# Block 2: when the low part of the next query's weights is made, and both modulation rows ahead of the first value pair

## What is computed

```python
for i in range(DEPTH_2):
    sh, sc, gt = jnp.split(jax.nn.silu(c) @ ada_w[i] + ada_b[i], 3, axis=-1)
    h = rms_norm(x, norm_g[i]) * (1.0 + sc[:, None]) + sh[:, None]
    u, z = jnp.split(h @ w_in, [n_mix_cols], axis=-1)
    o, oc = mixer(u, uc, ...)
    x = x + gt[:, None] * ((o * jax.nn.silu(z)) @ w_out)
```

## Time and profile before

| | us |
|---|---|
| median of 3 runs (lowest, highest) | 2190.47 (2190.22, 2192.97) |
| the profiled execution: time, span | 2195.91, 2194.1 |
| PE busy | 1974.0 (90%) |
| DVE busy | 1199.5 (55%) |
| ACT busy | 1098.0 (50%) |
| POOL busy | 985.2 (45%) |
| block 2, layers 0, 1, 2, 3: from, us | 935, 1209, 1577, 1963 |

### The profile page before, as it was taken

How to read it: one execution, slowest core, us unless ns; L and a number is a source line. 1 busy time by engine, 2 the same in 40 slices (tenths; PEclk the granted TensorE clock), 3 DMA queues, 4 the chain that set the end, 5 groups by cost and what they waited for, 6 DMA issues and landing times.

```text
span 2194.1 us, 39543 instructions
## 1 busy us (share of the span) xinstructions
PE 1974.0 (90%) x14720; PEld 1675.1 (76%) x14720; DVE 1199.5 (55%) x2584; ACT 1098.0 (50%) x2101; POOL 985.2 (45%) x616
## 2 busy tenths in 40 slices
PE   6899899998999899969998899899879989977897
PEld 5798789988898899946776697666569666656676
DVE  5854556657654466435775304677340766723574
ACT  5353465444543665454554526454443555644563
POOL 0474468303754485024453443344234545533563
PEclk8899999998999999979999999899999989989998
DMA  7343556564444565543112422322232211123222
GB/s 258 113 148 106 176 173 188 183 200 131 132 126 148 178 194 185 176 158 105 50 49 78 163 87 77 103 72 62 93 125 87 70 66 49 49 91 119 80 87 59
DMA packets 72994, 262.93 MB, mean 120 GB/s; under 512 B 8048, under 2 KB 10224, under 8 KB 72560
## 3 DMA queue, kind: packets, MB, share of 16 engines
q1 hardware_dynamic: 71536, 256.31, 36.5%
q0 software_dynamic: 1280, 4.20, 0.6%
HBM read 259.43 MB, written 1.05 MB: 119 GB/s over the span
## 4 chain that ended last, share of the span: by engine, by line
PE 67%; DVE 14%; issue 6%; ACT 6%; POOL 5%; DMA 1%; SPq 0%; DVEq 0%; ACTq 0%; POOLq 0%
PE gemm L494 16%; PE gemm L495 15%; PE gemm L496 15%; PE score L852 2%; DVE pr L1940 2%; DVE small L1903 2%; PE stat L739 2%; POOL w_parts L327 2%; PE obank L925 1%; PE gemm L792 1%; POOL rot L2124 1%; PE gemm L793 1%; PE gemm L794 1%; PE gemm L702 1%; ACT pr L1460 1%
## 5 line engine op out<-in xcount | busy, mean ns | idle before, releaser
L327 POOL TENSOR_TENSOR w_parts<-ring,w_parts 128x1024 fp32r<-128x1024 f32 x280 | 672.8, 2406 | 709.7 <-ACT w_parts L1112 698.7
L1112 ACT ACTIVATE w_parts<-ring 128x1024 fp32r<-128x1024 f32 x364 | 382.6, 1054 | 136.0 <-PE gemm L496 63.3
L494 PE MATMUL gemm<-g_hi,w_parts 128*128 128x256 f32 x1344 | 396.1, 295 | 28.5 <-DVE w_parts L327 10.7
L494 PE MATMUL gemm<-h_hi,w_parts 128*128 128x512 f32 (+1 forms) x928 | 379.8, 409 | 14.9 <-ACTq L1352 6.8
L495 PE MATMUL gemm<-g_lo,w_parts 128*128 128x256 f32 x1344 | 385.7, 287 | 0.0
L496 PE MATMUL gemm<-g_hi,w_parts 128*128 128x256 f32 x1344 | 385.1, 287 | 0.0
L495 PE MATMUL gemm<-h_lo,w_parts 128*128 128x512 f32 (+1 forms) x928 | 352.0, 379 | 0.0
L496 PE MATMUL gemm<-h_hi,w_parts 128*128 128x512 f32 (+1 forms) x928 | 351.5, 379 | 0.0
L494 PEld LDWEIGHTS gemm<-g_hi,w_parts 128*128 128x128 f32 x1344 | 265.4, 197 | 47.6 <-issue 24.0
L495 PEld LDWEIGHTS gemm<-g_lo,w_parts 128*128 128x128 f32 x1344 | 264.8, 197 | 0.1
L496 PEld LDWEIGHTS gemm<-g_hi,w_parts 128*128 128x128 f32 x1344 | 264.3, 197 | 0.0
(11 more groups left out here) (328 smaller groups left out, 3972.3 us busy)
## 6 DMA issues: line engine op xcount, KB each, us to landing
ring<-wall SPq DMA_DIRECT2D x478, 512.0 KB, 3.7
r<-nbias POOLq DMA_DIRECT2D x16, 256.0 KB, 3.0
cst<-consts SPq DMA_DIRECT2D x1, 2037.0 KB, 13.4
r<-x_t SPq DMA_DIRECT2D x1, 1024.0 KB, 5.7
x<-ctx_t SPq DMA_DIRECT2D x1, 1024.0 KB, 15.7
y_t<-x SPq DMA_DIRECT2D x4, 256.0 KB, 3.0
cst<-consts SPq DMA_DIRECT2D x1, 303.5 KB, 3.1
x<-pos SPq DMA_DIRECT2D x1, 128.0 KB, 2.1
```

What stands on the lines that cost most here:

```text
L327: eng.tensor_tensor(w_lo[:, at, :, :], ring[:, t % RING, :, :], w_hi[:, at, :, :].bitcast(F), ALU.subtract)\
L494: pe.matmul(out, w[0][:, k, :], x[0], start=start, stop=False)
L1112: act.activation(w_hi[:, at, :, :], ring[:, t % RING, :, :], ACT.Copy).then_inc(S["hi_ready"], 1)
```

## The change

1. `hi_parts` is called on ACT right behind the first pair's exponentials, for the query tile two ahead; before, that high part came with the query's copy at the second pair. Kinds A and B.
2. POOL waits before the low part of that tile until the first pair of the current chunk has been normalised.
3. In the last layer normalisation ACT no longer makes high parts of the two value tiles between the modulation rows; in layer 0 they come behind the exponential's square.
4. At the start of each layer all rows (two in layer 0, one after) are made ahead of value pair 0, in banks ob and tb and not in gemm banks, and so are the columns. ACT copies the rows behind the last high part of h. The first key sum and the first scores wait for the columns' copies.

The tile numbers, as a function that ACT and POOL share:

```diff
+        def qz_tile(L, i):
+            return AT["qz", L] + i + (4 if i >= 4 else 0) if FILL_SLOT[L] else AT["qz", L] + i + 1
```

On PE, in `block2`:

```diff
-                run(ada_row())
+                for r in range(FILL_RMS[L]):
+                    run(ada_row((ob, tb)[r]))
...
                     if j == 0:
-                        for _ in range(FILL_RMS[L] - 1):
-                            run(ada_row())
-                        for _ in range(FILL_RMS[L]):
-                            ada_columns()
+                        for r in range(FILL_RMS[L]):
+                            ada_columns((ob, tb)[r])
```

On ACT (`ada_columns_out` gets the same argument `at`):

```diff
-            def ada_row_out(ahead=AHEAD):
-                b = op(4, None, ahead)
+            def ada_row_out(ahead=AHEAD, at=None):
+                if at is None:
+                    b = op(4, None, ahead)
+                else:
+                    b = at
+                    n["tile"] += 4
+                    act.wait_ge(slot_used[(n["tile"] - 1) % RING], (n["tile"] - 1) // RING + 1)
...
                 for _ in range(FILL[i]):
-                    ada_row_out()
+                    ada_row_out(AHEAD if first else 0)
...
                 act.activation(zh[:, 0, :], rstd[:, :], ACT.Square).then_inc(S["rstd_ready"], 1)
+                if L == 0:
+                    hi_parts(n["tile"] + 1)
                 n["tile"] += 2
-                ada_row_out(0)
...
                     if L and m == KC - 3:
-                        hi_parts(n["tile"])
+                        hi_parts(n["tile"] + 4)
                 high(KC - 1)
+                for r in range(FILL_RMS[L]):
+                    ada_row_out(0, (ob, tb)[r])
...
                     if j == 0:
-                        for _ in range(FILL_RMS[L] - 1):
-                            ada_row_out()
-                        for _ in range(FILL_RMS[L]):
-                            ada_columns_out()
+                        for r in range(FILL_RMS[L]):
+                            ada_columns_out((ob, tb)[r])
...
                         exponential(c, u)
                         exponential(c, u + 1)
+                        if u == 0:
+                            hi_parts(qz_tile(L, 2 * c + 3))
```

On POOL, in `block2`:

```diff
                 def q_side(c):
-                    split_to(qz_tile(2 * c + 1) if c else AT["k", L] + 1)
+                    if c and kind != "C":
+                        pool.wait_ge(S["p_normed"], pbase(L) + (c - 1) * NU + 2)
+                    split_to(qz_tile(L, 2 * c + 1) if c else AT["k", L] + 1)
```

More of the change, by code:

```diff
@@ L762, in ones_head @@
                         pe.wait_ge(S["v_ready"], vbase(L) + nk)
+                        pe.wait_ge(S["ada_evac"], n["ada"])
                     if j == 1:
@@ L1121, in ada_row_out, with ada_columns_out @@
                 seq(ins)
-                act.sem_inc(S["bank_read"], 1)
+                if at is None:
+                    act.sem_inc(S["bank_read"], 1)
                 act.sem_inc(S["ada_row"], 1)
                 n["row"] += 1
-            def ada_columns_out():
+            def ada_columns_out(at=None):
                 r = n["ada"]
@@ L1129, in ada_columns_out @@
                 act.wait_ge(S["ada_col"], r + 1)
-                b = op(0)
+                b = op(0) if at is None else at
                 seq(act.activation(ada[:, :, :, :].rearrange("p l m v -> p (l m v)")[:, r * 8:(r + 1) * 8], b[:, 0:8], ACT.Copy))
-                act.sem_inc(S["bank_read"], 1)
+                if at is None:
+                    act.sem_inc(S["bank_read"], 1)
                 act.sem_inc(S["ada_evac"], 1)
@@ L2212, in block2 @@
                     pool.tensor_scalar(h2[:, m, T:N2], h2[:, m, T:N2], mod[:, m, 1:2], ada[:, L, m, 1:2], ALU.mult, ALU.add).then_inc(S["h_ctx"], 1)
-                def qz_tile(i):
-                    return AT["qz", L] + i + (4 if i >= 4 else 0) if FILL_SLOT[L] else AT["qz", L] + i + 1
                 def q_side(c):
-                    split_to(qz_tile(2 * c + 1) if c else AT["k", L] + 1)
+                    if c and kind != "C":
+                        pool.wait_ge(S["p_normed"], pbase(L) + (c - 1) * NU + 2)
+                    split_to(qz_tile(L, 2 * c + 1) if c else AT["k", L] + 1)
                     if kind != "B":
@@ L2244, in block2 @@
                 for c in range(KC):
-                    split_to(qz_tile(2 * c + 2))
+                    split_to(qz_tile(L, 2 * c + 2))
                     if not FILL_SLOT[L]:
```

## The result

The changed kernel takes 2171.08 us (median of five runs, 2169.15 to 2178.43) for 2190.47; the ratio is 0.9911, interval 0.9894 to 0.9927. Six more executions, beside 24 of the kernel before, gave a median of 2173.69 us and 0.9929 (0.9901 to 0.9957).

The account below looks back on a forecast made before the run. TensorE, busy for most of a chunk, was held by normalisation waits in layers 0 and 1 and a pause at layer 0's start. 2.0 + 5.5 + 3.3 + 2.4 = 13.2 us off 2190.47 gave 2177.3 us, range 2173.5 to 2183.5.

Parts of the forecast that it names:

- the start of layer 0: Both modulation rows first: squares 3.0 us earlier, value pair 0 later, no pause before query 0; −3.3 us together.
- the rival in which the clock returns early: Row matmuls lift PE's clock before value pair 0 in layer 0: 2.6 us more gain, 2174.7 us, chance 0.12.
- the columns: Layers 1 to 3: columns no longer wait 0.8 us for a copied gemm bank; −2.4 us in sum.
- which edit acts where: Attention loops: high part with low part behind bias loads in layer 1, both edits in layer 0, wait alone in chunk 1.
- The margin in layer 1: The second L1940 of a chunk ends 0.2 us before PE asks for it.
- the two loop terms: Gains from removed PE waits in the attention loops: 2.0 us in layer 0 and 5.5 us in layer 1.
- All six waits go (five of 0.2 and one of 0.9): −2.0 us: Layer 0's attention: PE's turn no longer waits for the normalisation; bounds 0 and 2.0 us.
- The five waits of 1.1 us go whole: −5.5 us: Layer 1's attention: PE's turn no longer waits for the second normalisation; bounds 2.8 and 5.5 us.
- the slower rival: Layer 3: low part released only by the second pair's normalisation, PE idles 3.1 us, clock falls; 2208 us, chance 0.03.
- the rivals with a gain: Early clock (0.12), slower ring at layer 0's start (0.13), layer 1's wait kept (0.06), loop edits without effect (0.03).
- the upper bound of both terms: Most the loop edits could gain: 2.0 us in layer 0, 5.5 us in layer 1.
- ACT's order doesn't change: Layer 3: only POOL's low part moves, 0.3 us later, covered by a gap of 3.1 us; cost 0.

Follow-up runs that it names:

- e2: The changed kernel with the attention loop of the kernel before, so only rows first, banks ob and tb, and columns: 2190.18 us, ratio 0.9996.
- e8: The changed kernel plus two extra VectorE operations between the second pair's two normalisations, chunks 2 to 6 of layer 1, so PE waits there again: 2175.35 us.
- e4: The kernel before with only POOL's wait for the first pair's normalisation added, the high part left at the second pair: 2187.55 us.
- e3: The kernel before with only ACT's high part moved to the first pair, without POOL's wait for the normalisation: 2180.90 us.
- e9: The changed kernel plus one extra VectorE operation between the second pair's two normalisations, chunks 2 to 6 of layer 1: 2170.62 us.
- e1: The kernel before with both attention loop edits (earlier high part, POOL's wait) and rows and columns as before: 2179.20 us, ratio 0.9957.
- e7: The changed kernel with POOL's low part in layer 3 waiting for the second pair's normalisation instead of the first's: 2191.16 us.

## Why the prediction was wrong

**Right: the start of layer 0, step by step.** Taken from the first square, which came 3.0 us earlier as forecast, nearly every time fits: the exponential's square 0.2 us before its forecast place, the low parts within 0.1, row tiles 2, 3 and 4 within 0.3. Tile 5 was 1.1 us late and all behind it with it, so value pair 0 started 29.3 us behind the first square for 28.1. The pair then ran 14.0 us to query 0 and not 15.0, since the clock returned after some 3.5 us: a little of the rival in which the clock returns early. That the two misses, 1.1 us late and 1.0 us early, cancelled was luck. In the second profile of the changed kernel that rival came true in full: the pair ran 12.0 us, all at full clock. Start of layer 0 as a whole: 3.0 us up to the first square and 0.2 from there to VectorE's first shuffle behind query 0 (50.8 us and 50.6), 3.2 in all, forecast 3.3. Between other profiles it varies: from the last normalisation's final pass to that shuffle it is 59.1 to 61.2 us in the five with the old start and 55.8 to 57.7 in the six with the new one, 2.9 between the means.

**Right in the first profiles: the columns,** 0.9, 0.5 and 0.8 us at the start of layers 1 to 3 (2.2, forecast 2.4). Between the means of two profiles each it is 0.3, 0.2 and 1.4. e2 shows that this is not safe where the clock falls later.

**Right: which edit acts where.** In layer 1 the high part alone, with the low part straight behind the bias loads; in layer 0 both; the wait alone in chunk 1. All eleven waits went. The margin in layer 1 was forecast as 0.2 us and is about nothing (the second L1955 ends at 1433.21, PE starts at 1433.26), but it held. What the Trainium skill says (SBUF — State Buffer, "SBUF: two separate sides") had been weighed there: by it the collision would only move to the first normalisation of the pair. That is what the trace shows, 1.13 us for 0.49.

**Wrong: the size of the two loop terms.** The failing steps are "All six waits go (five of 0.2 and one of 0.9): −2.0 us" and "The five waits of 1.1 us go whole: −5.5 us". The waits went whole, and gave 3.3 us (1.1 in chunk 1 and 0.43 in each of five) and 10.1 (the 11.0 of layer 1 less 0.9 for the columns, with the clock in it). I had taken the idle time of the waits for their price. Two things were missing.

First, the overlap that a wait breaks. PE's scores and turn in layer 0, chunk 4, before, and the same place after:

```profile
1111.56 1.13 PE L857 MATMUL score<-arena,d 64*128 64x256 f32 x8
1112.91 0.27 PE L885 MATMUL tbank<-cst,pr 64*128 64x64 f32 x1 [0.21 <-DVE pr L1940]
```

```profile
1100.38 1.14 PE L862 MATMUL score<-arena,d 64*128 64x256 f32 x8
1101.35 0.22 PE L890 MATMUL tbank<-cst,pr 64*128 64x64 f32 x1
```

From start to start it is 1.35 us with a wait that is shown as 0.21, and 0.97 without: the turn normally starts 0.17 us before the modelled end of the scores. The turn itself is 0.05 us longer behind a wait. So 0.21 us of idle time cost 0.43, and 1.11 in layer 1 cost 1.25 (chunk periods 20.83 to 20.40 and 22.36 to 21.11 us). Over eleven waits this makes 2.0 us.

Second, the clock. Layer 1 has 20 us at half clock for 34 or 37, and 10.1 less the 6.3 of waits and overlap leaves about 4 us for it. How much of that hangs on the removed waits differs between the profiles. In the second profile of before the clock fell behind four of the five turns with a wait, at 1.6 us each; in the first, only one of the lost spells stood there (at 1521 us), and 10 us more at half clock stood behind the rests of 2.94 and 2.47 us, which both kernels have. Over the four profiles with the waits it is 11 falls in 20 chunks, some 4.4 us per layer by 1.6 us each; without them it is none. I had charged the clock to long rests alone, at the start of layer 0 and in the slower rival, though the trace of before showed 0.57 behind that turn. e8 shows the link in the other direction. Why the rest of 2.94 us was followed by 10 us at half clock in two profiles (before, e4) and by 3.4 in all others is not shown.

2.0 + 4 is the 6 us by which the forecast fell short. By stages, from the means of two profiles each, with the forecast in brackets: last normalisation 2.6 us (3.0), layer 0 3.3 (2.3), layer 1 11.3 (6.3), layer 2 −0.5 (0.8), layer 3 2.6 (0.8). So layers 2 and 3 missed too, and cancelled. Of the rivals with a gain none had the loops' part; "clock returns early" was the right kind in the wrong place, and the range held nothing more for the loops, since I had put the upper bound of both terms at the idle time itself.

**Wrong, and hidden in the sum: "ACT's order doesn't change" in layer 3.** It does in the last chunk, where no query follows that could have brought the high part. The edit makes it at the first pair's exponentials, 16 to 19 us earlier, so PE's wait for the low part shrinks; but POOL's low part now runs beside four operations of VectorE and stretches them (four L1981 took 1.42 us together at 2150.57 us, the same four, now L1996, 3.58 at 2129.28, beside L327 from 2129.03 for 2.54), and PE waits longer for the output bank. PE's waits from there on, before (from 2152 us) and with the change (from 2129 us):

```profile
PE gemm L494 <- POOL w_parts L327: 5.0, 1, 5.0
PE obank L925 <- DVEq L1976: 2.2, 1, 2.2
```

```profile
PE obank L930 <- DVEq L1991: 5.3, 1, 5.3
PE gemm L498 <- POOL w_parts L327: 1.3, 1, 1.3
```

From the start of the wait for the output bank to the end of the kernel it is 38.9 us for 40.6 (means of two profiles), a gain of 1.7 that the forecast put at nothing. e3, with the high part alone, waits 1.4 us for the low part, e2 and e4 4.7 and 5.0.

**What is left open.** Layer 2 (no edit in its loop) differs by up to 6.5 us between runs (382.5 in e9, 389.0 in e1) and layer 3 by up to 6 (e7 apart), with spells of half clock in places with long rests; I did not follow those one by one. How much of a time rests on them shows in e2, where the stages say 2.5 us and the times nothing.

## What to carry to other kernels

A repeated wait of TensorE costs more than the idle time beside it: compare the start-to-start distance with and without it, and count what the granted clock loses in the chunks that have the wait. A bound from above that is set at the shown idle time is too low. Cut a long kernel into stages and compare stage by stage with two or more profiles of each kernel: here most stages repeated to 0.4 us between two profiles where whole executions differed by 12, but what no edit touched could still differ by several. And look at the last chunk of a loop by itself: its order can be another.

## What the runs showed of the hardware

Unexpected was that TensorE worked at two speeds at the same granted clock. The same 288 matmuls of 128x256 in layer 1, ahead of query 0, in the two profiles of the kernel before:

```profile
1269.30:1303.20 33.90, 33.90 (x289) 33.90 (x289) 0.00 (x0) 8.00 (x12) 11.94 (x5) 1.00 0.23 82
```

```profile
1255.57:1288.20 32.63, 32.63 (x288) 32.63 (x289) 0.00 (x0) 8.00 (x12) 11.94 (x5) 1.00 0.24 84
```

The clock reads 1.00 and PE is never idle in both, and it takes 33.90 us or 32.63: 117.7 or 113.3 ns each. The long products with 128x256 in block 1 do the same, a median of 118 or 113 ns from one start to the next, for some hundred microseconds at a time and independently of the edit. Between 300 and 420 us the two profiles of before read 118 and 113; the same instructions of ACT lie 7.0 us apart at the start of that stretch and 11.2 at its end, which is some 4 of the 12.5 us by which the profiles differ ahead of the last normalisation's final pass. The matmuls of 128x512 keep 233 or 234 ns in every run. What chooses the speed stays open.

Also new to me was how little rest it takes: a rest of 0.8 us beside the 0.56 that each chunk of 22 us has was followed by a fall behind some of the waits in e8, and the same rest of 2.94 us was followed by 10 us at half clock in one profile and by 3.4 in another of the same kernel. Nothing here says when a fall comes; the number of them is what a kernel can change.
